# The two layers' modulation: weights as the stationary operand instead of the conditions

## The chip, the cores and the metric

The kernel runs on one core of one Trainium2 chip. The metric is the device time of one execution in microseconds (us). All numbers come from that one core.

## What is computed

The model is two layers of a diffusion backbone over 384 tokens: 128 context tokens and 256 latent tokens. The part that matters here is the adaLN modulation, which every layer does ahead of its mixers:

```python
mod = jax.nn.silu(cond) @ ada_w[layer] + ada_b[layer]        # cond: (1024,), ada_w[layer]: (1024, 6144)
sh1, sc1, g1, sh2, sc2, g2 = jnp.split(mod[..., None, :], 6, axis=-1)
h = rms_norm(x, norm_g[layer, 0]) * (1.0 + sc1) + sh1
```

There are two conditions, one for the context tokens (`c_ctx`) and one for the latent tokens (`c`). So over both layers this is a product of a 2 x 1024 matrix with a 1024 x 12288 matrix, all in float32. The weights are 50 MB.

## The kernel before, in words

The kernel is a sequence of stages. A stage is a block in which each engine has its own program, and a block ends when all engines have ended it, so stages don't overlap. `modulation` is the first stage; it fills `cx.modT`, which holds the result with the output features on partitions: `modT[p, j, c]` is feature 128 j + p for condition c, with 96 values of j for two layers of 48. The stage after it is `norm`, which squares x on ScalarE, sums the squares on TensorE (L267, 8 matmuls with a matrix of ones) and scales with `modT`.

`modulation` walks through the weights in 24 tiles of 1024 x 512 (2 MB each), in a loop of 8 rounds with three tiles (`u` = 0, 1, 2) in each. There are three buffers `w[:, u]`, and each has a semaphore of its own for its load. In a round:

- SyncE (L192) issues the load of tile u once TensorE has finished the matmuls of the tile that was in this buffer (`summed`).
- TensorE (L204) multiplies for each of the three tiles: 8 matmuls over the 8 slices of 128 input features. The stationary operand is `sg[:, k, :]`, 128 x 2, the two conditions after SiLU; the moving operand is `w[:, u, k, :]`, 128 x 512. The result is a row per condition: 2 partitions x 512.
- ScalarE (L223) copies these two rows out of PSUM into `row`, a tile of 128 partitions that was cleared before (L229).
- TensorE (L210) turns the rows after the matmuls of all three tiles: 4 transposes of 128 x 128 for each tile, into `tr`.
- VectorE (L239) copies the 4 x 2 columns that hold values out of `tr` into `modT`.

After the loop VectorE adds the biases, adds 1 to the scales and multiplies by the norm's gains (L243 to L251).

Every matmul of plain float32 is two instructions of TensorE with two loads of the stationary operand: 8 matmuls for each of 24 tiles are the 384 records of L204. A transpose is one.

Further names that the prediction uses: `gla` is the stage of the gated linear attention (L690, L704 and L707 are its matmuls), `s5_prepare` a stage of the second layer (L1376 and L1381), L849 the product of queries and sub-keys in the expert retrieval, all plain float32.

Of the kernel before, what the change touches and what calls it, by code (L numbers as in the profile page):

```python
# [24 lines left out]
ACT = mybir.ActivationFunctionType  # L25
# [7 lines left out]
P = 128  # L33
D = 1024
KC = D // P
# [13 lines left out]
MODS = 6 * KC  # L49
# [114 lines left out]
def modulation(nc, sems, cx, d):  # L164


    NW = 3
    N = 2 * 12
    with Stage(nc, sems, "mod") as s:
        w = s.sb("w", [P, NW, KC, 512])  # L170
        bias, cond, sg, row = s.sb("bias", [P, 2, MODS]), s.sb("cond", [P, KC, 2]), s.sb("sg", [P, KC, 2]), s.sb("row", [P, NW, 512])
        normg = s.sb("normg", [P, 4, KC])
        one = s.sb("one", [P, 2, 2, KC, 2])
        acc, tr = s.ps("acc", [P, NW, 512]), s.ps("tr", [P, NW, 512])
        small, loaded = s.sem("small"), [s.sem(f"w{i}_loaded") for i in range(NW)]
        sig, silu = s.sem("sigmoid"), s.sem("silu")
        summed, copied, turned, stored = s.sem("summed"), s.sem("copied"), s.sem("turned"), s.sem("stored")
        own, cleared = s.sem("dve"), s.sem("rows_cleared")
        with nc.Block() as block:
            @block.sync  # L180
            def _(sp):
                sp.dma_start(cond[:], d["cond"]).then_inc(small, 16)
                sp.dma_start(cx.const[:], d["consts"][:, 0:C_KEEP]).then_inc(small, 16)
                sp.dma_start(bias[:], d["ada_b"]).then_inc(small, 16)
                sp.dma_start(normg[:], d["norm_g"]).then_inc(small, 16)
                sp.dma_start(cx.x[:], d["x"]).then_inc(small, 16)
                sp.dma_start(cx.finalg[:], d["final_g"]).then_inc(small, 16)
                with sp.Fori(0, N // NW) as i:
                    for u in range(NW):

                        sp.wait_ge(summed, i * NW + u + 1)
                        sp.dma_start(w[:, u], d["ada_w"][bass.ds(i * NW + u, 1)].rearrange("a p k n -> p (a k) n")).then_inc(loaded[u], 16)  # L192

            @block.tensor
            def _(pe):
                pe.sem_inc(summed, NW)
                pe.sem_inc(turned, NW)
                pe.wait_ge(silu, 1)
                with pe.Fori(0, N // NW) as i:
                    for u in range(NW):  # L200
                        pe.wait_ge(loaded[u], i * 16 + 16)
                        pe.wait_ge(copied, i * NW + u + 1)
                        for k in range(KC):
                            mm = pe.matmul(acc[0:2, u, :], sg[:, k, :], w[:, u, k, :], start=k == 0, stop=k == KC - 1)  # L204
                        mm.then_inc(summed, 1)
                    for u in range(NW):
                        pe.wait_ge(copied, i * NW + u + 1 + NW)
                        pe.wait_ge(stored, i * NW + u + 1)
                        for b in range(4):
                            mm = pe.transpose(tr[:, u, b * P:(b + 1) * P], row[:, u, b * P:(b + 1) * P], cx.ident)  # L210
                        mm.then_inc(turned, 1)

            @block.scalar
            def _(act):
                act.sem_inc(copied, NW)
                act.wait_ge(cleared, 1)
                act.wait_ge(small, 96)
                nc.scalar.activation(sg[:], cond[:], ACT.Sigmoid).then_inc(sig, 1)
                with act.Fori(0, N // NW) as i:
                    for u in range(NW):  # L220
                        act.wait_ge(summed, i * NW + u + 1 + NW)
                        act.wait_ge(turned, i * NW + u + 1)
                        nc.scalar.activation(row[0:2, u], acc[0:2, u, :], ACT.Copy).then_inc(copied, 1)  # L223

            @block.vector
            def _(dve):
                dve.sem_inc(stored, NW)
                st = Steps(dve, own)
                nc.vector.memset(row[:], 0.0).then_inc(cleared, 1)  # L229
                st.done(nc.vector.memset(cx.ones[:], 1.0))  # L230
                st.done(nc.vector.memset(cx.eps[:], EPS))
                dve.wait_ge(small, 96)
                st.done(nc.vector.tensor_copy(cx.iota[:], cx.const[:, C_IOTA:C_IOTA + P]))
                dve.wait_ge(sig, 1)
                nc.vector.tensor_tensor(sg[:], sg[:], cond[:], ALU.mult).then_inc(silu, 1)
                with dve.Fori(0, N // NW) as i:
                    for u in range(NW):
                        dve.wait_ge(turned, i * NW + u + 1 + NW)
                        nc.vector.tensor_copy(cx.modT[:, bass.ds((i * NW + u) * 4, 4), :],  # L239
                                              tr[:, u].rearrange("p (b c) -> p b c", b=4)[:, :, 0:2]).then_inc(stored, 1)  # L240
                dve.wait_ge(stored, N + NW)
                m = cx.modT[:]
                st.done(nc.vector.tensor_tensor(m, m, bias[:].rearrange("p l j -> p (l j)").unsqueeze(2).to_broadcast([P, 2 * MODS, 2]), ALU.add))  # L243
                st.settle()
                for l in range(2):
                    for h in range(2):
                        st.done(nc.vector.tensor_scalar(one[:, l, h], cx.mod(l, 3 * h + 1), 1.0, None, ALU.add))
                st.settle()
                for l in range(2):
                    for h in range(2):  # L250
                        st.done(nc.vector.tensor_tensor(cx.scale[:, l, h], one[:, l, h],  # L251
                                                        normg[:, 2 * l + h].unsqueeze(2).to_broadcast([P, KC, 2]), ALU.mult))
# [1632 lines left out]
def build(nc, d):  # L1885
    sems = Semaphores(nc)
    with Stage(nc, sems, "g") as g:
# [4 lines left out]
        cx.iota = g.sb("iota", [P, P], F16)  # L1892
        cx.ident = cx.const[:, C_ID:C_ID + P]
        modulation(nc, sems, cx, d)


# [145 lines left out]
```

## Time and profile before

| | us |
|---|---|
| median of 3 runs | 4067.95 (4067.78 to 4073.82) |
| span of the profiled execution | 4066.5 |
| TensorE matmul busy | 3353.7 (82%) |
| TensorE weight load busy | 2861.8 (70%) |
| VectorE busy | 2757.6 (68%) |
| ScalarE busy | 958.9 (24%) |
| GpSimd busy | 1262.1 (31%) |
| modulation, from the start to the last copy into `modT` | 193 |

The profiled execution is one execution; its span runs from the first to the last instruction. "PE" is TensorE's matmul, "PEld" its load of the stationary operand (which overlaps PE), DVE VectorE, ACT ScalarE, SPq the queue on which SyncE issues DMAs. PEclk is the granted clock of TensorE: 1.00 is 2.4 GHz, 0.50 is 1.2 GHz. A record of a matmul or of a load has a latency in it, so records in a row overlap: what one costs in a stream is the distance from one start to the next, not its duration.

### The profile page before, as it was taken

The numbers are of one execution on the slowest core, as the hardware profiler recorded it, in microseconds if no ns is written. First come the engines' busy times: TensorE is split into PE (matmuls) and PEld (weight loads), VectorE is DVE, ScalarE is ACT, GpSimd is POOL, SyncE is SP. The second block draws the span as 40 slices with busy tenths as digits, with TensorE's granted clock in tenths as the row PEclk, the third lists the DMA queues.
The fourth block names the chain that finished last, engine by engine and source line by source line (L and its number), as shares of the span: only waits on it lengthen the run. The fifth ranks groups of instructions, "written<-read, shape, count | busy, mean of one in ns | idle before, by whom it ended". The sixth has DMA issues, their size and how long they took to land. (4 is left out here: it accounts for less than half of the span.)

```text
span 4066.5 us, 63769 instructions
## 1 busy us (share of the span) xinstructions
PE 3353.7 (82%) x22510; PEld 2861.8 (70%) x22510; DVE 2757.6 (68%) x4082; ACT 958.9 (24%) x1677; POOL 1262.1 (31%) x727
## 2 busy tenths in 40 slices
PE   8976476998899899977975555779798999998788
PEld 1274256987788789865764454779787988996666
DVE  0043534699977677698546786449997776778965
ACT  0101201232222222222312111113222222222223
POOL 0000000364522222243512654007463232223443
PEclk9987558998999999999985677889899999999999
DMA  7531002232333333222410000233233333332232
GB/s 303 210 100 53 3 29 83 88 104 93 98 119 113 108 109 123 83 88 78 124 62 3 14 8 6 77 109 114 84 97 111 117 113 103 115 122 68 87 98 93
DMA packets 94125, 377.05 MB, mean 93 GB/s; under 512 B 11488, under 2 KB 12256, under 8 KB 90224
## 3 DMA queue, kind: packets, MB, share of 16 engines
q1 hardware_dynamic: 94064, 376.33, 27.8%
q8 instruction: 27, 0.44, 0.0%
q14 instruction: 34, 0.28, 0.0%
HBM read 373.86 MB, written 2.42 MB: 93 GB/s over the span
## 5 line engine op out<-in xcount | busy, mean ns | idle before, releaser
L1188 POOL TENSOR_TENSOR ex_ul<-ex_ur,ex_uh 128x512 fp32r<-128x512 f32 x384 | 547.5, 1446 | 1034.6 <-ACT ex_uh L1094 1034.6
L1230 PE MATMUL peer_acc<-ex_vh,ex_wh 128*128 128x512 f32 x1536 | 503.1, 409 | 51.6 <-DVE ex_wl L160 51.6
L929 POOL TENSOR_TENSOR ret_ul<-ret_ur,ret_uh 128x512 fp32r<-128x512 f32 x128 | 199.8, 1584 | 1073.4 <-ACT ret_uh L894 1073.3
L1216 PE MATMUL ex_s<-peer_hi,ex_uh 128*128 128x384 f32 x1536 | 522.1, 340 | 11.4 <-POOL ex_ul L1188 4.9
L1218 PE MATMUL ex_s<-peer_hi,ex_ul 128*128 128x384 f32 x1536 | 516.4, 336 | 0.0
L1217 PE MATMUL ex_s<-peer_lo,ex_uh 128*128 128x384 f32 x1536 | 515.8, 336 | 0.0
L1230 PE MATMUL peer_acc<-ex_vl,ex_wh 128*128 128x512 f32 x1536 | 480.8, 394 | 0.0
L1230 PE MATMUL peer_acc<-ex_vh,ex_wl 128*128 128x512 f32 x1536 | 479.7, 394 | 0.0
L1137 DVE TENSOR_TENSOR ex_o<-g_iota,peer_i1T 128x1536 f16<-128x1536 f16 x256 | 472.8, 1847 | 0.0
L1193 POOL TENSOR_TENSOR ex_vl<-ex_vr,ex_vh 128x1024 fp32r<-128x1024 f32 x128 | 326.2, 2550 | 394.6 <-ACT ex_vh L1098 394.6
L160 DVE TENSOR_TENSOR ex_vl<-ex_vr,ex_vh 128x1024 fp32r<-128x1024 f32 x128 | 276.5, 2160 | 179.4 <-ACT ex_vh L1098 179.4
L1098 ACT ACTIVATE ex_vh<-ex_vr 128x1024 fp32r<-128x1024 f32 x256 | 269.6, 1053 | 501.5 <-PE peer_acc L1230 458.6
L1230 PEld LDWEIGHTS peer_acc<-ex_vh,ex_wh 128*128 128x128 f32 x1536 | 273.4, 191 | 110.7 <-DVE ex_wl L160 31.7
L1230 PEld LDWEIGHTS peer_acc<-ex_vl,ex_wh 128*128 128x128 f32 x1536 | 292.3, 190 | 64.4
L1230 PEld LDWEIGHTS peer_acc<-ex_vh,ex_wl 128*128 128x128 f32 x1536 | 291.6, 190 | 63.9
L1135 DVE TENSOR_TENSOR ex_eq<-g_iota,peer_i2T 128x384 f16<-128x384 f16 x256 | 293.1, 1145 | 49.2 <-PEq L1236 47.6
L1216 PEld LDWEIGHTS ex_s<-peer_hi,ex_uh 128*128 128x128 f32 x1536 | 289.8, 189 | 20.3 <-issue 10.2
L1204 PEld LDWEIGHTS ex_s<-ex_oh,ex_o 128*128 128x128 f16 x3072 | 166.7, 96 | 194.1 <-DVE ex_ol L1141 176.0
L1204 PE MATMUL ex_s<-ex_oh,ex_o 128*128 128x32 f16 x3072 | 190.4, 177 | 134.9 <-DVE pe_A L1162 72.1
L1217 PEld LDWEIGHTS ex_s<-peer_lo,ex_uh 128*128 128x128 f32 x1536 | 290.0, 189 | 5.9
L1218 PEld LDWEIGHTS ex_s<-peer_hi,ex_ul 128*128 128x128 f32 x1536 | 289.7, 189 | 0.0
L160 DVE TENSOR_TENSOR ex_wl<-pe_A,ex_wh 128x384 fp32r<-128x384 f32 x128 | 187.5, 1466 | 142.5 <-ACT ex_wh L1101 140.3
(418 smaller groups left out, 5955.1 us busy)
## 6 DMA issues: line engine op xcount, KB each, us to landing
ex_vr<-in_peer_v SPq DMA_DIRECT2D x256, 512.0 KB, 3.7
ex_ur<-in_peer_u SPq DMA_DIRECT2D x192, 512.0 KB, 3.5
mod_w<-in_ada_w SPq DMA_DIRECT2D x24, 2048.0 KB, 7.6
ret_ur<-in_peer_u SPq DMA_DIRECT2D x64, 512.0 KB, 3.5
ql_w<-in_w_query SPq DMA_DIRECT2D x32, 512.0 KB, 3.7
in_w<-in_w_in SPq DMA_DIRECT2D x18, 512.0 KB, 3.5
out_w<-in_s_w_out SPq DMA_DIRECT2D x16, 512.0 KB, 3.6
val_w<-in_w_v SPq DMA_DIRECT2D x2, 2048.0 KB, 9.7
```

The costliest lines, as they stand in the source:

```text
L160: return nc.vector.tensor_tensor(r32(out), x, hi, ALU.subtract)
L929: nc.gpsimd.tensor_tensor(r32(ul[:, b, h]), ur[:, b, h], uh[:, b, h], ALU.subtract).then_inc(usplit, 1)
L1098: nc.scalar.activation(r32(vh[:, b]), vr[:, b], ACT.Copy).then_inc(vhigh, 1)
L1135: v.tensor_tensor(eq[:, b], cx.iota[:, gate * IB:gate * IB + IB].unsqueeze(1).to_broadcast(small), i2T[:, toks].unsqueeze(2).to_broadcast( ...
L1137: v.tensor_tensor(o1[:, b], cx.iota[:].unsqueeze(1).to_broadcast([P, TB, P]), i1T[:, toks].unsqueeze(2).to_broadcast([P, TB, P]), ALU.is_e ...
L1188: nc.gpsimd.tensor_tensor(r32(ul[:, b, h]), ur[:, b, h], uh[:, b, h], ALU.subtract).then_inc(usplit, 1)
L1193: nc.gpsimd.tensor_tensor(r32(vl[:, b]), vr[:, b], vh[:, b], ALU.subtract).then_inc(vsplit, 1)
L1204: pe.matmul(o, o1[:, b, t], oh[:, b, t], start=True, stop=False)
L1216: pe.matmul(o, r32(uh[:, b, k]), r32(hi[:, k]), start=k == 0, stop=False)
L1217: pe.matmul(o, r32(uh[:, b, k]), r32(lo[:, k]), start=False, stop=False)
L1218: mm = pe.matmul(o, r32(ul[:, b, k]), r32(hi[:, k]), start=False, stop=k == KC - 1)
L1230: mm = pe.matmul(acc[:, 2 * t + c, :], r32(lhs[:, b, w]), r32(rhs[:, b, c * 512:(c + 1) * 512]), start=False, stop=False, skip_group_check ...
```

## The change

The weights become the stationary operand, in pieces of 128 x 128, and the two conditions the moving operand. One tile is then 4 x 8 = 32 matmuls, each with 128 x 128 stationary and 128 x 2 moving, and the result has the output features on partitions: 128 x 2 for each of the four pieces b. The row copies on ScalarE, the tile `row` and its clearing, the transposes and the PSUM tile `tr` go, with their semaphores. VectorE copies 8 columns of `acc` into `modT` as soon as a tile is done. The loads of the weights from HBM, their order, the three buffers and the round of three tiles stay.

```diff
             def _(pe):
                 pe.sem_inc(summed, NW)
-                pe.sem_inc(turned, NW)
                 pe.wait_ge(silu, 1)
                 with pe.Fori(0, N // NW) as i:
                     for u in range(NW):
                         pe.wait_ge(loaded[u], i * 16 + 16)
-                        pe.wait_ge(copied, i * NW + u + 1)
-                        for k in range(KC):
-                            mm = pe.matmul(acc[0:2, u, :], sg[:, k, :], w[:, u, k, :], start=k == 0, stop=k == KC - 1)
-                        mm.then_inc(summed, 1)
-                    for u in range(NW):
-                        pe.wait_ge(copied, i * NW + u + 1 + NW)
                         pe.wait_ge(stored, i * NW + u + 1)
                         for b in range(4):
-                            mm = pe.transpose(tr[:, u, b * P:(b + 1) * P], row[:, u, b * P:(b + 1) * P], cx.ident)
-                        mm.then_inc(turned, 1)
+                            for k in range(KC):
+                                mm = pe.matmul(acc[:, u, 2 * b:2 * b + 2], w[:, u, k, b * P:(b + 1) * P], sg[:, k, :], start=k == 0, stop=k == KC - 1)
+                        mm.then_inc(summed, 1)
 
             @block.scalar
             def _(act):
-                act.sem_inc(copied, NW)
-                act.wait_ge(cleared, 1)
                 act.wait_ge(small, 96)
                 nc.scalar.activation(sg[:], cond[:], ACT.Sigmoid).then_inc(sig, 1)
-                with act.Fori(0, N // NW) as i:
-                    for u in range(NW):
-                        act.wait_ge(summed, i * NW + u + 1 + NW)
-                        act.wait_ge(turned, i * NW + u + 1)
-                        nc.scalar.activation(row[0:2, u], acc[0:2, u, :], ACT.Copy).then_inc(copied, 1)
 
             @block.vector
             def _(dve):
                 dve.sem_inc(stored, NW)
                 st = Steps(dve, own)
-                nc.vector.memset(row[:], 0.0).then_inc(cleared, 1)
                 ...
                 with dve.Fori(0, N // NW) as i:
                     for u in range(NW):
-                        dve.wait_ge(turned, i * NW + u + 1 + NW)
+                        dve.wait_ge(summed, i * NW + u + 1 + NW)
                         nc.vector.tensor_copy(cx.modT[:, bass.ds((i * NW + u) * 4, 4), :],
-                                              tr[:, u].rearrange("p (b c) -> p b c", b=4)[:, :, 0:2]).then_inc(stored, 1)
+                                              acc[:, u, 0:8].rearrange("p (b c) -> p b c", b=4)).then_inc(stored, 1)
```

## Rows read from the trace of the kernel before

**Rows 1.** Groups of instructions, 14 to 193.1 us: busy us, mean ns | idle before, releasers.
```profile
L204 PE MATMUL mod_acc<-mod_w,mod_sg 128*2 128x512 f32 x384 | 167.4, 596 | 14.2 <-DMA mod_w<-in_ada_w 14.2
L204 PEld LDWEIGHTS mod_acc<-mod_w,mod_sg 128*2 128x2 f32 x384 | 32.1, 85 | 143.2 <-issue 143.2
L210 PE MATMUL mod_tr<-g_const,mod_row 128*128 128x128 f32 x96 | 12.2, 277 | 0.0
```
**Rows 2.** SyncE's queue, 30 to 193 us: who waited for whom, us, times, longest.
```profile
SPq L192 <- PE mod_acc L204: 127.5, 19, 7.6
```
**Rows 3.** Busy us (x instructions) by stretch, then PEclk, DMA share, GB/s: modulation.
```profile
40.00:60.00 20.00, 20.00 (x56) 4.86 (x55) 0.33 (x2) 1.76 (x3) 0.00 (x0) 1.00 0.76 283
14.00:17.00 3.00, 2.85 (x4) 0.47 (x5) 0.00 (x0) 0.00 (x0) 0.00 (x0) 1.00 1.02 437
17.00:20.00 3.00, 3.00 (x8) 0.59 (x7) 0.00 (x0) 0.00 (x0) 0.00 (x0) 1.00 1.01 431
```
**Rows 4.** Timeline of modulation: start us, us, instruction, count [idle before].
```profile
14.15 22.08 PE L204 MATMUL mod_acc<-mod_w,mod_sg 128*2 128x512 f32 x48 [14.15 <-DMA mod_w<-in_ada_w]
...
59.13 0.17 DVE L239 COPY g_modT<-mod_tr 128x8 f32 x1 [21.10 <-PE mod_tr L210]
...
81.28 0.17 DVE L239 COPY g_modT<-mod_tr 128x8 f32 x1 [21.11 <-PE mod_tr L210]
...
192.92 0.17 DVE L239 COPY g_modT<-mod_tr 128x8 f32 x1 [0.27 <-PE mod_tr L210]
```
**Rows 5.** Timeline of two bursts of L1381 in s5_prepare, and what reads the result.
```profile
2158.32 1.86 PEld L1381 LDWEIGHTS s5p_pb<-g_const,s5p_U 48*128 48x128 f32 x16 [1.55 <-ACT s5p_U L1357]
...
2166.70 3.48 PEld L1381 LDWEIGHTS s5p_pb<-g_const,s5p_U 48*128 48x128 f32 x16 [1.59 <-ACT s5p_U L1357]
...
2166.86 0.33 PEld L1381 LDWEIGHTS s5p_pb<-g_const,s5p_U 48*128 48x128 f32 x1
...
2169.85 0.33 PEld L1381 LDWEIGHTS s5p_pb<-g_const,s5p_U 48*128 48x128 f32 x1
...
2170.49 0.28 ACT L1362 ACTIVATE s5o_uc<-s5p_pb 128x128 f32 x1 [3.85 <-PE s5p_pb L1381]
```
**Rows 6.** The two bursts by stretch (columns as rows 3), and L1381's durations min/median/max in ns.
```profile
2158.30:2160.20 1.90, 1.87 (x16) 1.86 (x16) 1.80 (x12) 0.00 (x0) 0.00 (x0) 1.00 0.00 0
2166.70:2170.20 3.50, 3.50 (x16) 3.48 (x16) 3.40 (x11) 0.00 (x0) 0.00 (x0) 0.50 0.01 2
...
L1381 PEld LDWEIGHTS s5p_pb<-g_const,s5p_U x128: 183/330/335, 2158.3 to 2228.0; 48*128 48x128 f32 x128
L1381 PE MATMUL s5p_pb<-g_const,s5p_U x128: 271/410/446, 2158.3 to 2228.1; 48*128 48x48 f32 x128
```
**Rows 7.** The gla stage by stretch (columns as rows 3), 520 to 570 us.
```profile
520.00:570.00 50.00, 50.00 (x215) 43.88 (x216) 5.39 (x20) 1.47 (x3) 0.00 (x0) 0.50 0.00 0
```
**Rows 8.** Timeline of loads in the gla stage (matmuls of L704: 128 x 64 moving).
```profile
518.87 0.93 PEld L704 LDWEIGHTS gla_ob<-gla_am,l_v 128*128 128x128 f32 x4 [0.22 <-DVE gla_am L778]
519.92 0.93 PEld L707 LDWEIGHTS gla_ob<-gla_qd,gla_S 64*128 64x128 f32 x4
```
**Rows 9.** L849 (128 x 128 stationary, 128 x 128 moving) by stretch, columns as rows 3.
```profile
756.00:760.00 4.00, 4.00 (x18) 4.00 (x19) 0.00 (x0) 1.81 (x4) 1.33 (x2) 0.50 0.43 173
760.00:765.50 5.50, 5.50 (x47) 5.50 (x47) 2.65 (x14) 3.40 (x6) 1.18 (x1) 0.91 0.35 98
```
**Rows 10.** TensorE in the norm stage at both clocks, by stretch, columns as rows 3.
```profile
193.00:201.00 8.00, 5.43 (x16) 2.96 (x16) 1.28 (x10) 4.91 (x10) 0.00 (x0) 1.00 0.00 0
650.30:658.20 7.90, 7.79 (x16) 4.12 (x16) 0.00 (x0) 2.91 (x8) 0.00 (x0) 0.69 0.00 0
```
**Rows 11.** Timeline of L1204 and L1205, float16: the second adds to the first's columns.
```profile
930.92 0.19 PE L1204 MATMUL ex_s<-ex_oh,ex_o 128*128 128x32 f16 x1
930.95 0.19 PE L1205 MATMUL ex_s<-ex_ol,ex_o 128*128 128x32 f16 x1
930.97 0.19 PE L1204 MATMUL ex_s<-ex_oh,ex_o 128*128 128x32 f16 x1
```

More of the change, by code:

```diff
@@ L170, in modulation @@
         w = s.sb("w", [P, NW, KC, 512])
-        bias, cond, sg, row = s.sb("bias", [P, 2, MODS]), s.sb("cond", [P, KC, 2]), s.sb("sg", [P, KC, 2]), s.sb("row", [P, NW, 512])
+        bias, cond, sg = s.sb("bias", [P, 2, MODS]), s.sb("cond", [P, KC, 2]), s.sb("sg", [P, KC, 2])
         normg = s.sb("normg", [P, 4, KC])
         one = s.sb("one", [P, 2, 2, KC, 2])
-        acc, tr = s.ps("acc", [P, NW, 512]), s.ps("tr", [P, NW, 512])
+        acc = s.ps("acc", [P, NW, 512])
         small, loaded = s.sem("small"), [s.sem(f"w{i}_loaded") for i in range(NW)]
         sig, silu = s.sem("sigmoid"), s.sem("silu")
-        summed, copied, turned, stored = s.sem("summed"), s.sem("copied"), s.sem("turned"), s.sem("stored")
-        own, cleared = s.sem("dve"), s.sem("rows_cleared")
+        summed, stored, own = s.sem("summed"), s.sem("stored"), s.sem("dve")
         with nc.Block() as block:
```

## The prediction

> **What bounds the kernel now.** Only the first stage changes, so I read that stage alone, and ask first whether it waits for its 50 MB or for TensorE. The groups of the stretch answer it: TensorE's matmuls of L204 are busy 167.4 us, the transposes of L210 another 12.2 us, and the one time that TensorE waited for a DMA is the 14.2 us ahead of the first tile [rows 1]. The queue of the loads says the same from its side: from 30 us on it waited 19 times, 127.5 us in all, for L204 to give a buffer back [rows 2]. In the table by stretch TensorE is busy 20.00 of 20 us with the DMA engines at 0.76 and 283 GB/s; while the first tiles come, with nothing to wait for, the DMAs move 437 GB/s [rows 3]. So TensorE sets the pace. The timeline gives the pace: from the first copy of one round to that of the next, 81.28 - 59.13 = 22.15 us for three tiles, 7.38 us for a tile; the first matmul starts at 14.15 us and the last copy into `modT` ends at 192.92 + 0.17 = 193.09 us [rows 4]. 192 matmuls are 384 records; 16 records a tile, mostly 0.43 us apart, are 6.9 us, and turning the rows is the rest.
>
> **What the change removes.** On the path: the transposes and the waits around them, 7.38 - 6.9 = 0.5 us a tile, and the 384 records with 512 moving columns. Off the path: 24 row copies on ScalarE and the clearing of `row`, which runs while the small inputs load. Both are worth nothing of their own. The loads of the weights keep their number, size and order on SyncE's queue. They are now released by a `summed` that comes at another pace, and 2 MB at 437 GB/s take 4.8 us, so they stay covered whatever TensorE needs above that (without that cover a tile could not go below 4.8 us). VectorE's copy keeps its size (128 x 8) and waits for the matmuls directly; behind it on VectorE nothing is queued but the next copy, and TensorE waits for it only three tiles later, so it costs nothing until the last tile.
>
> **What it adds.** 32 matmuls a tile, each two records, each with a full load of 128 x 128 float32: 64 pairs of load and matmul for a tile, 24 x 64 = 1536 in all, against 384. So the question is the distance from one pair to the next when nearly nothing is streamed. No instruction before streams 2 columns, so I bound it. The nearest rows are L1381: 48 x 128 stationary, 48 columns moving, plain float32, 16 pairs in a burst. One burst is at the clock of 1.00, the other at 0.50 [rows 6]. At 1.00 it takes 1.86 us from the first load to the end of the last; less one load (the minimum of 183 ns) over 15 distances that is 0.112 us a pair. At 0.50 the second load starts at 2166.86 and the sixteenth at 2169.85: 2.99 / 14 = 0.2136 us a pair [rows 5]. The two differ by the ratio of the clocks, which are 1.2 and 2.4 GHz: a pair is 256 cycles. For 48 rows and 128 rows the load costs the same: in the gla stage four loads of 128 x 128 take 0.93 us, (0.93 - 0.33) / 3 = 0.20, with a first distance that is shorter as it is in L1381 [rows 8]. Fewer columns can't shorten this, since the 128 columns of the load are what takes the time (at 48 moving columns the matmul is the shorter of the two). So I take 256 cycles. Below lies nothing that the trace shows for a float32 load; above lies the gla stage, where from the first of four pairs to the first of the next four it is 519.92 - 518.87 = 1.05 us and not 4 x 0.2136 = 0.85, 0.2 us for each change of group [rows 8]. There the number of rows changes from 128 to 64; here it never does, so I take nothing, and keep as upper end 0.2 us for each of the 96 accumulation groups, 19 us.
>
> That eight matmuls in a row add to the same two columns costs nothing by the rows either: L1205 adds to the 32 columns that L1204 has just written, and these start 0.03 us apart [rows 11], far closer than 0.11.
>
> **The clock decides the sign.** At 0.112 us, 64 pairs are 7.2 us, just under the 7.38 of now. At 0.2136 they are 13.7 us. The stage before ran at full clock from 17.2 us on: until then the first records were twice as far apart, 4 of them in 2.85 us, then 8 in 3.00 us [rows 3]. They streamed 512 columns after a load of 2. What does the clock do when the stream is nearly all loads? Two stretches stand beside each other. L849 starts at 0.50, each full load followed by 128 moving columns; the clock is 0.50 for the first 4 us and 0.91 on average over the next 5.5 us [rows 9]. The gla stage has TensorE busy 50.00 of 50 us, loads busy 43.88 us of it, moving columns 64 or 128 to a load, and the clock is 0.50 throughout [rows 7]. Loads in close order did not raise it there. The new stream has the same loads with 2 columns behind each. It is on the gla side and beyond it, and it starts from a TensorE that has been idle. I take 0.50 for the whole stage.
>
> The Trainium skill, "TensorE: Matmul & The Clock Gate", in its section on the HAM clock gate, says the throttle depends on how busy TensorE has been and that sustained activity releases it. If a row of loads counts as being busy, this change would run at 2.4 GHz; that is the first rival below. The gla stretch, busy in every microsecond by the record and at 1.2 GHz, speaks against that reading.
>
> **The sum,** against the span of 4066.5 us, which lies 1.45 us under the median:
> - The first pair starts at 14.15 us as now (it waits for the same load). 1535 distances x 0.2136 = 327.9 us, so the last load starts at 342.0 us.
> - From a burst's last load to the first reader of its result: 2170.49 - 2169.85 = 0.64 us [rows 5]; the copy takes 0.17 us. The last copy ends at 342.9 us, against 193.09: +149.8 us.
> - What is late next: biases and scales follow as now, then the norm stage. Its 16 records on TensorE took 5.43 us because modulation left the clock at 1.00; the norm that starts at 0.50 takes 7.79 us [rows 10]. +2.4 us, since ScalarE's root waits for them. The stages behind it begin after tens of us without matmuls as before: no change.
> - +152.2 us in all. 4067.95 + 152.2 = 4220 us, 3.7% slower. The loads from HBM are then a third busy and wait for TensorE.
>
> **The rivals.**
> 1. *The clock rises all the same (the other side: not slower).* For it: TensorE is never idle, and the short bursts of L1381 do run at 1.00 when it was up already. Against it: gla. The time: about 3 us at 0.50 first as now (14 pairs, 1.4 us lost), so 14.15 + 1535 x 0.112 + 1.4 + 0.5 + 0.17 = 188.1 us, 5.0 us less, 4063 us. The trade is decided at 7.38 / 64 = 0.115 us a pair: below it the change gains. 4063 is within 0.2% (8.1 us) of before, about what a measurement of this kernel can tell from no change; only with no cold start and no distance above 256 cycles would it gain 0.2%.
> 2. *The clock is up for a part of the stage,* in turns. Halfway is 4220 - 79 = 4141 us. For it: the clock did go up and down between the bursts of s5_prepare [rows 6], but those have other matmuls between them. Here the stream is the same from the first tile to the last, so I see no reason for a change within it.
> 3. *Each accumulation group costs the gap of gla:* 96 x 0.2 = 19 us more, 4239 us. If it came with every four records it would be 384 x 0.2 = 77 us, 4297 us.
> 4. *Load and matmul don't overlap.* Then a pair at the low clock is 0.33 + 0.41 = 0.74 us [rows 6], 1536 of them 1137 us, and the time about 5030 us. The records speak against it: the loads of L1381 are 0.33 us long and start 0.2136 us apart, with matmuls of 0.41 us between them. The Trainium skill, "TensorE: Matmul & The Clock Gate", in the section on packing small matmuls, says that a load overlaps a matmul in flight only when the row groups differ; here they are the same rows, and so they are in L1381, where the trace shows an overlap of the records.
>
> **How the numbers follow.** Low clock throughout with 256 cycles a pair: 0.80, 4220 us, give or take 8 for the distance (0.2133 to 0.215 us) and small costs at the 8 turns of the loop. Rival 3: 0.06. Rival 2: 0.04. Rival 1: 0.09, of which 0.07 within 0.2% and 0.02 faster. Rival 4: 0.01. The range of 4212 to 4240 holds the first and the milder form of rival 3, 0.85, and leaves out the rest. Slower by over 0.2%: 0.91.
>
> **What would show it.** The groups of the stage: L204's loads x1536 at 330 ns each with PEclk at 0.50 in every stretch from 14 to 342 us; starts 0.213 us apart across the borders of b, u and of the rounds; 13.7 us from copy to copy on VectorE; SyncE's queue waiting about 6 us longer for each buffer; DMA near 150 GB/s. The 16 records of the first norm at 7.8 us. The prediction is wrong if PEclk is 1.00 after the first few us (then copies come 7.2 us apart), or if the starts are even but farther apart than 256 cycles (then 2 columns have a cost that 48 don't show).

## The result, and the profile after

The changed kernel takes 4225.85 us (median of 4 runs, 4222.73 to 4227.27) against 4069.16 for the kernel before in the same comparison: 1.038 times as long, with a 95% interval of 1.0366 to 1.0396. In a second comparison it was 4221.54 against 4069.82, 1.0368 (1.0351 to 1.0385). The span of the profiled execution is 4224.4 us.

The groups of instructions of the first two stages, modulation and norm, in the changed kernel (columns as in [rows 1]):

```profile
L203 PE MATMUL mod_acc<-mod_sg,mod_w 128*128 128x2 f32 x1536 | 327.8, 353 | 14.3 <-DMA mod_w<-in_ada_w 14.3
L203 PEld LDWEIGHTS mod_acc<-mod_sg,mod_w 128*128 128x128 f32 x1536 | 327.8, 333 | 14.3 <-issue 14.3
L252 PE MATMUL n_ss<-n_sq,g_ones 128*128 128x384 f32 x16 | 8.0, 676 | 2.6 <-ACT n_sq L259 2.6
L224 DVE COPY g_modT<-mod_acc 128x8 f32 x24 | 4.0, 167 | 328.6 <-PE mod_acc L203 328.6
```

1536 loads and 1536 matmuls stand where 384 stood, and TensorE is busy with them for 327.8 us without a pause; a record of a load is 333 ns long. The timeline of VectorE gives the pace, a copy every 13.65 us, and the end of the stage (start us, us, instruction, idle before):

```profile
192.08 0.17 DVE L224 COPY g_modT<-mod_acc 128x8 f32 x1 [13.48 <-PE mod_acc L203]
205.74 0.17 DVE L224 COPY g_modT<-mod_acc 128x8 f32 x1 [13.49 <-PE mod_acc L203]
219.39 0.17 DVE L224 COPY g_modT<-mod_acc 128x8 f32 x1 [13.49 <-PE mod_acc L203]
...
342.27 0.17 DVE L224 COPY g_modT<-mod_acc 128x8 f32 x1 [13.49 <-PE mod_acc L203]
```

13.65 us / 64 pairs = 0.2133 us a pair (one load and its matmul), with nothing left over at the borders of pieces, tiles or rounds. The last copy ends at 342.44 us; before it ended at 193.09 [rows 4].

By stretch (us, then busy us (x instructions) of PE, PEld, DVE, ACT, POOL, then PEclk, DMA share, GB/s):

```profile
17.00:20.00 3.00, 3.00 (x15) 3.00 (x16) 0.00 (x0) 0.00 (x0) 0.00 (x0) 1.00 1.02 437
20.00:40.00 20.00, 20.00 (x95) 20.00 (x95) 0.17 (x1) 0.00 (x0) 0.00 (x0) 1.00 0.42 165
100.00:120.00 20.00, 20.00 (x95) 20.00 (x95) 0.17 (x1) 0.00 (x0) 0.00 (x0) 1.00 0.44 172
345.00:360.00 15.00, 7.71 (x16) 3.87 (x15) 6.57 (x5) 4.36 (x9) 0.00 (x0) 0.89 0.00 0
```

What SyncE's queue waited for from 20 to 350 us (us, times, longest):

```profile
SPq L191 <- PE mod_acc L203: 282.6, 21, 22.3
```

The DMA engines fall from a share of 0.76 [rows 3] to 0.42 to 0.44; the queue waits 282.6 / 21 = 13.5 us for each buffer against 127.5 / 19 = 6.7 [rows 2]. But PEclk stands at 1.00 in all rows of the modulation (only the last row, of the norm stage, reads less), although loads of 333 ns, 0.2133 us apart, are what the burst at 0.50 showed [rows 5, 6]. So either the column is wrong here, or a pair with 2 columns costs 512 cycles at 2.4 GHz. The trace of after can't settle that, and the experiments begin with it.

### The profile page after: what moved, and what is told of

Read it like the earlier page. It is cut to its first block and busy times, and to the rows that moved or that the text cites. A ratio compares the mean times of both kernels' runs of the same rounds, so it can differ in the third digit from the quotient of the medians.

```text
span 4224.4 us, 65740 instructions
## 1 busy us (share of the span) xinstructions
PE 3511.0 (83%) x23566; PEld 3150.5 (75%) x23566; DVE 2758.1 (65%) x4081; ACT 945.3 (22%) x1653; POOL 1271.4 (30%) x727
## 5 line engine op out<-in xcount | busy, mean ns | idle before, releaser
L1173 POOL TENSOR_TENSOR ex_ul<-ex_ur,ex_uh 128x512 fp32r<-128x512 f32 x384 | 557.2, 1471 | 1028.6 <-ACT ex_uh L1079 1028.6
L203 PE MATMUL mod_acc<-mod_sg,mod_w 128*128 128x2 f32 x1536 | 327.8, 353 | 14.3 <-DMA mod_w<-in_ada_w 14.3
L203 PEld LDWEIGHTS mod_acc<-mod_sg,mod_w 128*128 128x128 f32 x1536 | 327.8, 333 | 14.3 <-issue 14.3
```

Source lines behind the costliest of these rows:

```text
L203: mm = pe.matmul(acc[:, u, 2 * b:2 * b + 2], w[:, u, k, b * P:(b + 1) * P], sg[:, k, :], start=k == 0, stop=k == KC - 1)
L1173: nc.gpsimd.tensor_tensor(r32(ul[:, b, h]), ur[:, b, h], uh[:, b, h], ALU.subtract).then_inc(usplit, 1)
```

## The experiments

Theory A, that of the prediction: a pair of load and matmul is the 256 cycles of its float32 load (0.2133 us at 1.2 GHz), and the clock stays at 1.2 GHz. Theory B: the column is right, the clock is at 2.4 GHz, and pairs with so few columns take 512 cycles.

**A warm start.** The changed kernel, with dense matmuls of 128 x 512 on constant data ahead of the stream (in part; what is not shown sets up the tiles `dump` and `fill`):

```diff
                 pe.sem_inc(summed, NW)
+                pe.wait_ge(filled, 1)
+                for n in range(12):
+                    pe.matmul(dump[:], fill[:, 0:P], fill[:], start=True, stop=True)
                 pe.wait_ge(silu, 1)
```

> The changed kernel, with 12 dense float32 matmuls of 128 x 512 on constant data ahead of it, while TensorE has nothing to do but wait for the first weights. Theory A: the clock is up when the stream of loads begins, so its first pairs are 0.107 to 0.112 us apart, and fall back to 0.213 us after some us; a gain of 1 to 5 us, 4221 to 4225 us. Theory B: pairs are 0.213 us apart from the first one; 4226 us.

4213.93 us in the one run. The stream's loads and the clock by stretch (us, PEld busy (x), PEclk, DMA share, GB/s):

```profile
14.40:16.20 1.80, 1.80 (x17) 1.00 1.02 437
16.50:18.20 1.70, 1.70 (x17) 1.00 1.04 443
20.00:24.00 4.00, 4.00 (x20) 0.50 0.70 295
```

All engines over the move of the clock (columns as above), and then the durations of the loads, min/median/max in ns:

```profile
18.00:20.00 2.00, 2.00 (x16) 2.00 (x17) 0.00 (x0) 0.00 (x0) 0.00 (x0) 0.79 1.03 442
20.00:24.00 4.00, 4.00 (x20) 4.00 (x20) 0.01 (x1) 0.00 (x0) 0.00 (x0) 0.50 0.70 295
```

```profile
L207 PEld LDWEIGHTS mod_acc<-mod_sg,mod_w x1536: 186/333/333, 14.4 to 337.4; 128*128 128x128 f32 x192
```

17 loads fall into 1.80 us and 17 into 1.70 (one by one the starts are 0.111 to 0.112 us apart), and the shortest is 186 ns long: with 2 moving columns a pair at 2.4 GHz takes 0.112 us (268 cycles), not the 0.2133 us that 512 cycles would be. Between 18 and 20 us the clock falls, and from there to the end of the stage PEclk reads 0.50 and the loads are 0.213 us apart, 20 of them in 4 us. So B falls, and with it the column: in this trace, where the clock had gone up and come down, it reads 0.50 for just those distances at which the trace of after reads 1.00. What is common to the places where it misleads is that the clock had not moved since the start of the profile: the stage in after, and the first records of before [rows 3]. There it reads 1.00, whatever the level. The last copy ends at 338.02 + 0.17 = 338.19 us, 4.3 us sooner than in after; the 44 pairs ahead of the fall saved 44 x (0.2133 - 0.1115) = 4.5 us, less the 0.1 us by which the stream began later. The rest of the gain of 7.6 us against the second comparison's 4221.54 is behind the stage; most of it lies at the last norm, which comes up again below.

**What keeps the clock down.** Three kernels change one thing, the number of moving columns behind each load: the two conditions are repeated in a tile `wide`, and the first two columns of each piece of the result are copied out. With 128 (in part; what is not shown declares and fills `wide`):

```diff
-                                mm = pe.matmul(acc[:, u, 2 * b:2 * b + 2], w[:, u, k, b * P:(b + 1) * P], sg[:, k, :], start=k == 0, stop=k == KC - 1)
+                                mm = pe.matmul(acc[:, u, 128 * b:128 * (b + 1)], w[:, u, k, b * P:(b + 1) * P], wide[:, k, :], start=k == 0, stop=k == KC - 1)
...
-                                              acc[:, u, 0:8].rearrange("p (b c) -> p b c", b=4)).then_inc(stored, 1)
+                                              acc[:, u, 0:512].rearrange("p (b c) -> p b c", b=4)[:, :, 0:2]).then_inc(stored, 1)
```

> 64 moving columns instead of 2 (the two conditions repeated 32 times, the first two result columns are copied out). Theory A (a pair is the 256 cycles of its load, and the clock stays at 1.2 GHz as long as hardly anything streams behind the loads): the load of 128 columns is still the longer part, so a pair is 0.213 us at the low clock, and the stage has now what the gla stage has, which stayed low: 4226 us. Theory B (the granted clock is 2.4 GHz as the table by stretch says, and a pair with so few columns takes 512 cycles): no shorter than 0.213 us, 4226 us or more.

> 128 moving columns instead of 2: 64 times the streaming for the same result. Theory A: the stream is now that of L849, where the clock rose after some us, and load and matmul are 256 cycles each and overlap; a pair is 0.213 us at first and 0.107 to 0.112 us after that, the modulation ends at 187 to 190 us, the time is 4063 to 4067 us. Theory B: more columns can't make a pair shorter; 4226 us or more.

> 96 moving columns, between the 64 at which the clock stayed low in this stage and the 128 at which it rose. Theory A says nothing on which side it is: 4220 to 4226 us if the clock stays low, 4064 to 4069 us if it rises, and nothing between unless the clock moves within the stage.

| moving columns | time, us | the stage's last copy ends |
|---|---|---|
| 2 | 4221.54 (4 runs) | 342.2 |
| 64 | 4224.69 (1 run) | 342.4 |
| 96 | 4063.62 (1 run) | 188.9 |
| 128 | 4067.45 (10 runs) | 188.1 |

The row with 96 comes from another comparison, in which the kernel before took 4069.45; in that of the others it took 4069.82.

64 columns, by stretch; then 128 columns, by stretch and VectorE's copies:

```profile
20.00:40.00 20.00, 20.00 (x96) 20.00 (x95) 0.17 (x1) 0.00 (x0) 0.00 (x0) 1.00 0.42 162
300.00:320.00 20.00, 20.00 (x96) 20.00 (x96) 0.33 (x2) 0.00 (x0) 0.00 (x0) 1.00 0.28 105
```

```profile
14.00:17.00 3.00, 3.00 (x14) 3.00 (x15) 0.00 (x0) 0.00 (x0) 0.00 (x0) 1.00 1.01 431
17.00:20.00 3.00, 3.00 (x24) 3.00 (x24) 0.00 (x0) 0.00 (x0) 0.00 (x0) 1.00 0.98 421
20.00:40.00 20.00, 20.00 (x182) 20.00 (x181) 0.50 (x3) 0.00 (x0) 0.00 (x0) 1.00 0.77 285
```

```profile
180.78 0.17 DVE L227 COPY g_modT<-mod_acc 128x8 f32 x1 [6.98 <-PE mod_acc L204]
187.92 0.17 DVE L227 COPY g_modT<-mod_acc 128x8 f32 x1 [6.98 <-PE mod_acc L204]
```

With 64 columns 96 matmuls fall into 20 us; with 128 it is 14 in the first 3 us and 182 in 20 us later on, a copy every 7.14 us: 0.1116 us a pair. The same 1536 loads, 64 times the streaming, and the stage is 154 us shorter than with 2 columns. At 128 and at 96 the distances fell from 0.213 to 0.112 us at 18 to 19 us, at 64 and at 2 they never did, and 0.2133 and 0.1116 us are also the distances of `warm_start` at 0.50 and at 1.00: what differs is the level of the clock. Whether this change costs 152 us or nothing that can be measured hung on it: with the clock up, the changed orientation is as fast as the old one (4067.45 against 4069.82, ratio 0.9993, 0.9983 to 1.0002). Its stage is then 5 us shorter [rows 4]; in the trace some 3 us of that are lost again in the stages behind, whose instructions are the same. With 2 columns the high clock was seen for the 44 pairs of `warm_start` alone; no run held it there for the whole stage.

The Trainium skill, "TensorE: Matmul & The Clock Gate", in its section on the HAM clock gate, has the clock follow how busy TensorE has been. The traces agree only in part: the matmul records cover 20.00 of 20 us both in the rows with 64 columns, which stayed at 1.2 GHz, and in the row with 128, which ran at 2.4 GHz, so the busy time of the profile does not tell them apart.

**The same pairs, a quarter of them.** The kernel leaves six of the eight slices out of the sum; all weights are still loaded.

```diff
-                            for k in range(KC):
-                                mm = pe.matmul(acc[:, u, 2 * b:2 * b + 2], w[:, u, k, b * P:(b + 1) * P], sg[:, k, :], start=k == 0, stop=k == KC - 1)
+                            for k in range(2):
+                                mm = pe.matmul(acc[:, u, 2 * b:2 * b + 2], w[:, u, k, b * P:(b + 1) * P], sg[:, k, :], start=k == 0, stop=k == 1)
```

> The changed kernel with 2 of the 8 slices of input features multiplied (the other 6 are left out of the sum; all 24 tiles are still loaded): 16 pairs a tile. Theory A: 16 x 0.213 = 3.4 us of TensorE a tile, less than the load of 2 MB from HBM; the stage is then bound by the loads, 4.8 us a tile at the 437 GB/s of the first us: 14 + 23 x 4.8 + 4 = 128 us for the modulation, about 4009 us. If the price were not per pair but per tile or per group, it would be longer than that.

4017.07 us in the one run. Copies on VectorE and a stretch of the stage:

```profile
121.22 0.17 DVE L224 COPY g_modT<-mod_acc 128x8 f32 x1 [4.73 <-PE mod_acc L203]
126.11 0.17 DVE L224 COPY g_modT<-mod_acc 128x8 f32 x1 [4.73 <-PE mod_acc L203]
130.99 0.17 DVE L224 COPY g_modT<-mod_acc 128x8 f32 x1 [4.71 <-PE mod_acc L203]
```

```profile
40.00:60.00 20.00, 14.70 (x67) 14.38 (x68) 0.67 (x4) 0.00 (x0) 0.00 (x0) 1.00 1.01 428
```

The pace is now 4.89 us a tile at 428 GB/s, with TensorE waiting for the DMAs: a price per tile or per group would have stayed, so it was per pair, and below it lies the floor of the loads. The estimate of 4.8 us from the first microseconds came out at 4.89 for the whole stage. It also says what the kernel before leaves lying: 7.38 - 4.89 = 2.5 us a tile, 60 us in all.

**A version that beats both.** If TensorE's streaming is the bound before, and a matmul with 2 stationary columns uses a sixty-fourth of the array, then four of them can share it. The kernel before, with the eight slices dealt to four column groups:

```diff
                         for k in range(KC):
-                            mm = pe.matmul(acc[0:2, u, :], sg[:, k, :], w[:, u, k, :], start=k == 0, stop=k == KC - 1)
+                            g = 32 * (k % 4)
+                            mm = pe.matmul(acc[g:g + 2, u, :], sg[:, k, :], w[:, u, k, :], start=k < 4, stop=k >= 4)
...
-                        nc.scalar.activation(row[0:2, u], acc[0:2, u, :], ACT.Copy).then_inc(copied, 1)
+                        for g in (0, 32, 64, 96):
+                            cp = nc.scalar.activation(row[g:g + 2, u], acc[g:g + 2, u, :], ACT.Copy)
+                        cp.then_inc(copied, 1)
...
-                        nc.vector.tensor_copy(cx.modT[:, bass.ds((i * NW + u) * 4, 4), :],
-                                              tr[:, u].rearrange("p (b c) -> p b c", b=4)[:, :, 0:2]).then_inc(stored, 1)
+                        nc.vector.tensor_reduce(cx.modT[:, bass.ds((i * NW + u) * 4, 4), :],
+                                                tr[:, u].rearrange("p (b g c) -> p b c g", b=4, g=4)[:, :, 0:2, :], X_AXIS, ALU.add).then_inc(stored, 1)
```

> The kernel before (conditions stationary, weights moving), but the 8 matmuls of a tile go in turn to four column groups of the array: the results of slices k and k + 4 land on partitions 32 (k mod 4) and the one after, so four matmuls, which use 2 columns of the array each, can run at the same time. ScalarE copies four pieces of two rows, the transposes are as before, and VectorE adds the four groups as it copies. If the four run side by side, TensorE needs 6.9 / 4 = 1.7 us and 0.5 us of turning a tile, the stage is bound by the loads at 4.8 us a tile, and the modulation ends at about 130 us: 4007 us, better than both kernels. If they run one after the other, 7.4 us a tile as before: 4069 us.

4014.33 us (4010.69 to 4021.81, 4 runs) against 4069.45: ratio 0.987, 0.9854 to 0.9887. Its timeline within one tile and from the last tile's matmuls to the last copy, and then a stretch:

```profile
63.33 0.11 PEld L205 LDWEIGHTS mod_acc<-mod_w,mod_sg 128*2 128x2 f32 x8 [3.76 <-ACT mod_row L225]
63.33 1.90 PE L205 MATMUL mod_acc<-mod_w,mod_sg 128*2 128x512 f32 x16 [2.84 <-DMA mod_w<-in_ada_w]
63.76 0.11 PEld L205 LDWEIGHTS mod_acc<-mod_w,mod_sg 128*2 128x2 f32 x4 [0.32 <-issue]
64.19 0.11 PEld L205 LDWEIGHTS mod_acc<-mod_w,mod_sg 128*2 128x2 f32 x4 [0.32 <-issue]
65.38 2.38 ACT L225 ACTIVATE mod_row<-mod_acc 2x512 f32<-2x512 f32 x4 [2.35 <-PE mod_acc L205]
...
126.94 3.30 PE L205 MATMUL mod_acc<-mod_w,mod_sg 128*2 128x512 f32 x16 [2.98 <-DMA mod_w<-in_ada_w]
...
130.39 2.39 ACT L225 ACTIVATE mod_row<-mod_acc 2x512 f32<-2x512 f32 x4 [3.90 <-PE mod_acc L205]
...
133.66 0.19 DVE L242 TENSOR_REDUCE g_modT<-mod_tr 128x32 f32 x1 [2.04 <-PE mod_tr L211]
```

```profile
80.00:100.00 20.00, 12.30 (x81) 3.95 (x82) 0.57 (x3) 9.77 (x17) 0.00 (x0) 0.83 1.00 426
```

Loads come four at a time every 0.43 us, where one came every 0.43 us before: the four groups run side by side, and 16 matmul records take 1.90 us. The stage runs at the floor of the loads (426 GB/s, 4.89 us from tile to tile); its clock moves up and down (0.83 in this stretch), which TensorE has the time for until the last tile; and the last copy ends at 133.85 us instead of 193.09. The expected 130 was 3.9 us too early: 23 distances of 4.89 us instead of 4.8 are 2.1 of it, and the last tile's matmuls, which waited for their load until 126.94, ran at the low clock (loads 0.8 us apart instead of 0.43) and took 3.30 us instead of 1.90, with nothing left to hide that behind. The Trainium skill, "TensorEngine Tiling (Array Packing)", in the section on the theoretical speedup, gives up to 4 times for a small dimension of at most 32; for float32 with 2 columns in each group this trace shows it, four records in the 0.43 us of one. Since the stage has reached its loads, the four groups can't show more here.

**The rest of the difference.**

> The changed kernel again, beside the others of this group. Both theories: 4226 us, with the modulation's last copy at 342.4 us. The first trace has 5.8 us more than the modulation and the first norm explain; they came in the S5 scan (2.6 us) and in the last norm (2.7 us). If the change causes them they are there again at the same places; if they come from the moment at which the clock happens to move, they are not, or elsewhere.

4221.54 us, span 4219.9. Laying the first starts of some 25 groups of the two kernels side by side: in the first trace of after they are 151.6 to 152.7 us later than before from the first norm's end to the beginning of the S5 scan, but for three groups inside the expert retrieval; at the end of the scan 155.0, and 157.9 behind the last norm. In the second trace they are 149.1 us later at the modulation's last copy, 150.9 behind the first norm (which lost 1.8 us here, and 2.6 in the first trace), 150.4 a few stages on and 150.2 to 150.3 at the end of the S5 scan, so the 2.6 us of the scan are gone; behind the last norm they are 153.4. The last norm shows the clock in both; this is its matmul in the first trace of after, then in before, then in `warm_start` (durations min/median/max in ns, first and last start):

```profile
L252 PE MATMUL fin_ss<-fin_sq,g_ones x16: 486/760/1006, 4201.4 to 4209.1; 128*128 128x384 f32 x16
```

```profile
L267 PE MATMUL fin_ss<-fin_sq,g_ones x16: 486/486/590, 4046.2 to 4051.1; 128*128 128x384 f32 x16
```

```profile
L257 PE MATMUL fin_ss<-fin_sq,g_ones x16: 486/486/590, 4191.9 to 4196.8; 128*128 128x384 f32 x16
```

It began at the low clock in both traces of after (matmuls of up to 1006 and 1009 ns) and at the high one in before. The instructions ahead of it are the same in both kernels. `warm_start` and `move64` have the change's loads too, at the low clock for nearly the whole stage, and there the last norm ran at the high clock (590 and 591 ns at most). So the change does not force it. What sets the level at that moment stays open.

## Why the prediction was right, point by point

- *What bounds the stage before:* right, TensorE and not the loads. `two_slices` and `four_groups` show the floor of the loads at 4.89 us a tile, under the 7.38 of before.
- *The distance of a pair:* right at both levels: 0.2133 us in after against the 0.2136 that was taken, and 0.1116 us in `move128` (0.111 to 0.112 in `warm_start`) against 0.112. It came from bursts with 48 rows and 48 columns; neither number mattered. The reading as 256 cycles holds at 1.2 GHz; 0.1116 us at 2.4 GHz are 268 cycles, so the two don't quite differ by the ratio of the clocks. The sum used the measured distances and is not touched by it.
- *The clock:* right, and for the stated reason. The gla stretch [rows 7], with 64 columns behind four loads of five, was the better neighbour than L849 with 128 [rows 9]: `move64` and `move128` set nearly these two streams into this stage, and they went the same two ways. Which of the two would decide was a judgement between two rows, and it was held at 0.80, not as certain.
- *The sum:* the last copy was put at 342.9 us and ended at 342.44; the first norm was put at +2.4 us and lost 2.6: its records took 8.0 us instead of 7.8. The forecast of both together was 152.2, and the first trace shows 152.0 behind the first norm. The median moved by 156.7, in the second comparison by 151.7. The span of the first trace grew by 157.9; what it has over the forecast is nearly all in the 5.8 us at the S5 scan and the last norm, which the sum had at nothing. "The stages behind it: no change" is thus the weakest step. In the second trace the 2.6 us of the scan were gone, the first norm lost only 1.8 us, and the last norm took 3 us more: that the 151.7 lies so near to the sum of 152.2 is in part luck.
- *The rivals:* the rising clock was put at 4063 us; with 96 or 128 columns behind each load it gives 4063.62 and 4067.45. A clock that is up for a part of the stage (rival 2) isn't there either: the copies of after are 13.65 us apart to the last, and in `warm_start` the clock fell once and stayed down. The gap between groups from gla (rival 3) isn't there: 64 pairs are 13.65 us with four groups in them. What it is in gla was not tried. That loads and matmuls don't overlap (rival 4) is out: at 0.112 us a pair, a load record of 186 ns and a matmul record of 251 ns can only stand in each other's time.
- *What would show it:* one point was wrong. PEclk was to read 0.50 through the stage; it read 1.00. By the first half of the text's own test ("wrong if PEclk is 1.00 after the first few us") a reader would have rejected a right prediction; only its second half, the distance of the copies (13.65 us and not 7.2), and the `warm_start` run put that straight. The rows of before held the warning: PEclk 1.00 from 14 to 17 us with records twice as far apart [rows 3].

## What to carry to other kernels

When a product has a narrow side, count what TensorE does per weight: here a stationary float32 piece of 128 columns took 0.112 us at the high clock, about as much as streaming 128 columns did before (512 took 0.43), so making the wide operand stationary saves nothing, and with 2 columns behind each load it ran at the low clock, at which the pairs are 1.9 times as far apart. What gained was to keep the wide operand moving and to put four narrow matmuls side by side into column groups, until the loads from HBM set the pace. Judge the clock by the distances of like instructions at two places, not by the clock column alone where it hasn't moved yet.

## What the runs showed that was not expected

- More streaming made the kernel faster: 128 moving columns instead of 2, for the same result, took 154 us off (4221.54 to 4067.45).
- PEclk reads 1.00 from the start of the profile until the clock first moves, whatever its level is (0.2133 us a pair at "1.00" in after, the same distance at "0.50" in `warm_start`).
- The 2 MB loads hold 426 to 430 GB/s until the last of them once nothing holds them back (before: 283; after: 105 to 172).
